# Two more key units of the first layer among the experts, and cross-attention weights forward in the ring

## The reference

```python
# first block, one layer
u = modulate(rmsnorm(h, g_norm1), sh1, sc1)
h = h + ga1 * hybrid_mixer(u, ...)               # convolution branch and gated linear attention
u2 = modulate(rmsnorm(h, g_norm2), sh2, sc2)
h = h + ga2 * hierarchical_moe(u2, ...)          # 32 experts: (silu(t @ w1) * (t @ w3)) @ w2, two a row
x = modulate(rmsnorm(h, g_final), shf, scf)
# second block, for each of its two layers l
x = x + 0.5 * swiglu_ffn(rms_norm(x, ffn1_norm_g[l]), ...)
proj = rms_norm(x, mix_norm_g[l]) @ w_mix_in[l]  # rwkv7_time_mix and moba_attention on its columns
x = x + concatenate([y_rwkv, y_moba]) @ w_mix_out[l]
# memory_cross_attention; mem_n = rms_norm(mem, mem_norm_g[l]), mem is an input of 256 rows
q = rms_norm(x, xattn_norm_g[l]) @ w_q[l]
k, v = jnp.split(mem_n @ w_kv[l], 2, axis=-1)    # 4 heads of 256
x = x + (softmax(q @ k.T / 16) @ v) @ w_o[l]
x = x + 0.5 * swiglu_ffn(rms_norm(x, ffn2_norm_g[l]), ...)
```

## Time and profile before

| | us |
|---|---|
| median of 3 runs | 2267.16 (2261.84 to 2268.1) |
| the profiled execution | 2264.74 |
| its span in the trace | 2262.9 |
| TensorE busy (PE) | 2182.5, 96% of the span |
| TensorE weight load (PEld) | 1481.2, 65% |
| VectorE (DVE) | 1240.8, 55% |
| ScalarE (ACT) | 424.7, 19% |
| GpSimd (POOL) | 47.5, 2% |

### The profile page before, as it was taken

How to read it: one execution, slowest core, us unless ns; L and a number is a source line. 1 busy time by engine, 2 the same in 40 slices (tenths; PEclk the granted TensorE clock), 3 DMA queues, 4 the chain that set the end, 5 groups by cost and what they waited for, 6 DMA issues and landing times.

```text
span 2262.9 us, 29955 instructions
## 1 busy us (share of the span) xinstructions
PE 2182.5 (96%) x12564; PEld 1481.2 (65%) x12564; DVE 1240.8 (55%) x2258; ACT 424.7 (19%) x852; POOL 47.5 (2%) x79
## 2 busy tenths in 40 slices
PE   7999999999999889999999999999999999999998
PEld 5778853333333338857978768857884966687873
DVE  2798432100011146667576766676666867667675
ACT  1123321100000012101232321102210132322110
POOL 1000100000000000000000000000000000000000
PEclk9999999999999999999999999999999999999999
DMA  9656579999999985444341435436443441245441
GB/s 406 266 225 257 223 212 381 422 421 421 422 422 421 422 323 174 161 167 171 123 154 50 149 126 182 155 124 223 161 175 130 168 150 57 78 150 183 159 181 42
DMA packets 174716, 499.94 MB, mean 221 GB/s; under 512 B 7016, under 2 KB 99448, under 8 KB 144384
## 3 DMA queue, kind: packets, MB, share of 16 engines
q1 hardware_dynamic: 170416, 481.23, 56.4%
q0 software_dynamic: 4032, 16.43, 2.3%
q10 hardware_dynamic: 144, 0.52, 0.1%
HBM read 491.34 MB, written 6.82 MB: 220 GB/s over the span
## 4 chain that ended last, share of the span: by engine, by line
PE 84%; DMA 12%; DVE 2%; issue 1%; ACT 0%; SPq 0%; POOL 0%; DVEq 0%; POOLq 0%
PE bank L2487 23%; PE bank L2535 11%; DMA ring<-in_w 10%; PE bank L939 6%; PE bank L2600 6%; PE bank L1512 6%; PE bank L3030 2%; PE bank L1553 2%; PE bank L2848 2%; PE bank L3103 2%; PE bank L2705 2%; PE bank L1602 1%; PE bank L2711 1%; PE bank L929 1%; PE bank L1043 1%; PE bank L1074 1%
## 5 line engine op out<-in xcount | busy, mean ns | idle before, releaser
L2487 PE MATMUL bank<-Tw,Sx 128*128 128x256 f32 x1032 | 229.9, 379 | 0.0
L2487 PEld LDWEIGHTS bank<-Tw,Sx 128*128 128x128 f32 x1032 | 193.0, 190 | 24.6
L1969 DVE TENSOR_TENSOR sg<-sg,bank 128x512 f32<-128x512 f32 x16 | 11.0, 687 | 273.7 <-PE bank L1512 273.7
L2487 PE MATMUL bank<-ring,xT 128*128 128x256 f32 x688 | 155.5, 379 | 0.0
L2487 PEld LDWEIGHTS bank<-ring,xT 128*128 128x128 f32 x688 | 130.5, 190 | 18.0 <-issue 0.5
L939 PE MATMUL bank<-xT,ring 128*128 128x256 f32 x640 | 141.8, 380 | 0.0
L1512 PE MATMUL bank<-ring,xg 128*64 128x512 f32 x512 | 115.0, 595 | 23.7 <-DMA ring<-in_w 23.7
L939 PEld LDWEIGHTS bank<-xT,ring 128*128 128x128 f32 x640 | 120.7, 190 | 19.0 <-issue 3.3
L1512 PE MATMUL bank<-more,xg 128*64 128x512 f32 x512 | 115.1, 596 | 16.8 <-DMA more<-in_w 16.0
L1553 PE MATMUL bank<-ring,hTg 128*64 128x512 f32 x512 | 113.5, 595 | 0.0
L3527 DVE TENSOR_TENSOR whole<-bank,part 128x256 f32<-128x256 f32 (+1 forms) x133 | 57.4, 432 | 99.4 <-PE bank L2487 98.1
(11 more groups left out here) (640 smaller groups left out, 3679.2 us busy)
## 6 DMA issues: line engine op xcount, KB each, us to landing
ring<-in_w SPq DMA_DIRECT2D x128, 1024.0 KB, 23.6
ring<-in_ffn_w_in SPq DMA_DIRECT2D x88, 1024.0 KB, 7.7
ring<-in_first_pieces SPq DMA_DIRECT2D x33, 2048.0 KB, 12.8
more<-in_w SPq DMA_DIRECT2D x64, 1024.0 KB, 23.5
ring<-in_ffn_w_out SPq DMA_DIRECT2D x20, 2048.0 KB, 7.8
ring<-in_w_mix_in SPq DMA_DIRECT2D x12, 2048.0 KB, 7.8
ring<-in_xattn_w_kv SPq DMA_DIRECT2D x6, 2048.0 KB, 8.0
ring<-in_w_mix_out SPq DMA_DIRECT2D x4, 2048.0 KB, 15.9
```

The lines of the kernel that those rows point to most:

```text
L2487: last = nc.tensor.matmul(bank[BANK_OF[name]][:, 0:SEQ], lhs(k), rhs(k), start=(k == 0), stop=(k == 3))
```

## The change

Units 0 and 1 of layer 0 are made in loop steps 1 and 2 of the experts, and layer 1's four key units move from steps 2 to 5 to steps 3 to 6. `LEFT` becomes [2, 3, 6, 7] in layer 0 and stays [4, 5, 6, 7] in layer 1. The key and value pieces that are left take the first two of their four places in the ring (24 and 25) in both layers, each piece's columns taken from `LEFT`, and 26 and 27 are skipped. There is a DRAM buffer of keys and one of values for each layer, in place of one of values, one of keys and one of early keys; the early units go to the layer's buffer, and the layer's own store writes only the columns that it made. Both buffers of a layer are read as before.

```diff
-EARLY = ((1, 0, 2), (1, 1, 3), (1, 2, 4), (1, 3, 5))
+EARLY = ((0, 0, 1), (0, 1, 2), (1, 0, 3), (1, 1, 4), (1, 2, 5), (1, 3, 6))
...
-        k_dram = nc.dram_tensor("cross_keys", (P, KD * SEQ), F32)
-        k_early = nc.dram_tensor("early_keys", (P, KD * SEQ), F32)
-        v_dram = nc.dram_tensor("cross_values", (P, NT * D), F32)
-        v_rows = v_dram.ap().rearrange("p (t d) -> p t d", t=NT)
+        k_dram = [nc.dram_tensor(f"cross_keys{l}", (P, KD * SEQ), F32) for l in range(DEPTH_2)]
+        v_dram = [nc.dram_tensor(f"cross_values{l}", (P, NT * D), F32) for l in range(DEPTH_2)]
+        v_rows = [v_dram[l].ap().rearrange("p (t d) -> p t d", t=NT) for l in range(DEPTH_2)]
...
-                if l == 1:
-                    pool.dma_start(k_early.ap()[:, g * 512:(g + 1) * 512], flat(early_out)).then_inc(early_moved, 16)
+                if g < 4:
+                    pool.dma_start(k_dram[l].ap()[:, g * 512:(g + 1) * 512], flat(early_out)).then_inc(early_moved, 16)
...
         def skipped(l, j):
-            return (j in J_SKIPPED or (l, j) == (0, J_VALUES)
-                    or J_KV <= j < J_KV + 4 and not any(cross_left(l, g) for g in (2 * (j - J_KV), 2 * (j - J_KV) + 1)))
+            return j in J_SKIPPED or J_KV + len(LEFT[l]) // 2 <= j < J_KV + 4
...
-                    sp.wait_ge(kv_psum, kv_done(l, 2 * (j - J_KV) + 1))
+                    sp.wait_ge(kv_psum, kv_done(l, LEFT[l][2 * (j - J_KV) + 1]))
...
-                mid += [(a["xattn_w_kv_2"], 512 * n, 512) for n in range(4)]
+                mid += [(a["xattn_w_kv_2"], 512 * (LEFT[l][2 * n] // 2 if 2 * n < len(LEFT[l]) else 0), 512)
+                        for n in range(4)]
...
-                if KEYS_LEFT[l]:
-                    pool.wait_ge(kv_act, kv_done(l, 3))
+                keys, values = LEFT[l][:KEYS_LEFT[l]], LEFT[l][KEYS_LEFT[l]:]
+                if keys:
+                    pool.wait_ge(kv_act, kv_done(l, keys[-1]))
                     pool.sem_inc(pool_passed, 1)
-                    pool.dma_start(k_dram.ap(), flat(k_out[:, :, :])).then_inc(k_stored, 16)
+                    pool.dma_start(k_dram[l].ap()[:, keys[0] * 512:(keys[-1] + 1) * 512],
+                                   flat(k_out[:, 2 * keys[0]:2 * keys[-1] + 2, :])).then_inc(k_stored, 16)
...
-                pool.dma_start(flat(kx[:, :, :]), (k_dram if KEYS_LEFT[l] else k_early).ap()).then_inc(kv_loaded, 16)
-                pool.dma_start(flat(vx[:, :, :]), v_dram.ap()).then_inc(kv_loaded, 16)
+                pool.dma_start(flat(kx[:, :, :]), k_dram[l].ap()).then_inc(kv_loaded, 16)
+                pool.dma_start(flat(vx[:, :, :]), v_dram[l].ap()).then_inc(kv_loaded, 16)
...
-                s = wait_piece2(pe, J_KV + g // 2, l)
+                s = wait_piece2(pe, J_KV + LEFT[l].index(g) // 2, l)
```

More of the change, by code:

```diff
@@ L157 @@
 EARLY_SEGMENTS = [_s for _s in _full if _s[0] < _s[1]]
-EARLY_COLUMNS = [(_l, _g * 256 if _g < 4 else D + 512 + (_g % 2) * 256) for _l, _g, _ in EARLY]
+EARLY_COLUMNS = [(_l, _g * 256 if _g < 4 else D + (_g // 2 - 2) * 512 + (_g % 2) * 256) for _l, _g, _ in EARLY]
 EARLY_LAYERS = list(dict.fromkeys(_l for _l, _, _ in EARLY))
@@ L824, in pool1 @@
             pool.wait_ge(kv_act, 2)
-            pool.dma_start(v_rows[:, :, 0:512], v_out[:, :, 0:512]).then_inc(v_stored, 16)
+            pool.dma_start(v_rows[0][:, :, 0:512], v_out[:, :, 0:512]).then_inc(v_stored, 16)
             pool.wait_ge(bd_stored, 16)
@@ L829, in pool1 @@
                 pool.wait_ge(early_act, u + 2 + EARLY_LAYERS.index(l))
-                if l == 1:
-                    pool.dma_start(k_early.ap()[:, g * 512:(g + 1) * 512], flat(early_out)).then_inc(early_moved, 16)
-                else:
-                    c = 512 + (g % 2) * 256
-                    pool.dma_start(v_rows[:, :, c:c + 256], early_out).then_inc(early_moved, 16)
+                if g < 4:
+                    pool.dma_start(k_dram[l].ap()[:, g * 512:(g + 1) * 512], flat(early_out)).then_inc(early_moved, 16)
+                else:
+                    c = (g // 2 - 2) * 512 + (g % 2) * 256
+                    pool.dma_start(v_rows[l][:, :, c:c + 256], early_out).then_inc(early_moved, 16)
         def tensor1(pe):
@@ L2042, in build @@
         J_SKIPPED = (51,)
-        J_VALUES = J_KV + 2
         assert PER_LAYER % SLOTS == 0 and J_MIX == FB + N_DOWN
@@ L2054, in build @@
         KEYS_LEFT = [sum(g < 4 for g in t) for t in LEFT]
-        assert all(n in (0, 4) for n in KEYS_LEFT)
+        assert all(t[0::2] == [g - 1 for g in t[1::2]] for t in LEFT)
         def keys_stored(l):
@@ L2410, in pool2 @@
                 norm_rstd(pool, l * 4 + 5)
-                if KEYS_LEFT[l]:
-                    pool.wait_ge(kv_act, kv_done(l, 3))
+                keys, values = LEFT[l][:KEYS_LEFT[l]], LEFT[l][KEYS_LEFT[l]:]
+                if keys:
+                    pool.wait_ge(kv_act, kv_done(l, keys[-1]))
                     pool.sem_inc(pool_passed, 1)
-                    pool.dma_start(k_dram.ap(), flat(k_out[:, :, :])).then_inc(k_stored, 16)
-                if len(LEFT[l]) > KEYS_LEFT[l]:
-                    pool.wait_ge(kv_act, kv_done(l, 7))
+                    pool.dma_start(k_dram[l].ap()[:, keys[0] * 512:(keys[-1] + 1) * 512],
+                                   flat(k_out[:, 2 * keys[0]:2 * keys[-1] + 2, :])).then_inc(k_stored, 16)
+                if values:
+                    pool.wait_ge(kv_act, kv_done(l, values[-1]))
                     pool.sem_inc(pool_passed, 1)
-                    columns = slice(512 if l == 0 else 0, D)
-                    pool.dma_start(v_rows[:, :, columns], v_out[:, :, columns]).then_inc(v_stored, 16)
+                    columns = slice((values[0] // 2 - 2) * 512, (values[-1] // 2 - 1) * 512)
+                    pool.dma_start(v_rows[l][:, :, columns], v_out[:, :, columns]).then_inc(v_stored, 16)
                 pool.wait_ge(k_stored, keys_stored(l))
```

## The result

The changed kernel takes 2270.37 us (median of 14 runs, 2267.72 to 2275.25), the kernel before 2266.62 us (14 runs, 2261.84 to 2269.9): ratio 1.0022, 95% interval 1.0014 to 1.0029. The forecast was 2260.0 with a range up to 2267. On a second chip, in experiment e5, the ratio was 1.0026 (1.0016 to 1.0036). So the change costs 4 to 6 us where 7 were to be gained.

A forecast was written before the change was run, and what follows sets the result against it. The DMA was taken to bound the expert stage (TensorE busy 96% overall). Terms 6.4 - 10.7 - 3.4 + 0.5 = -7.2 us took the profiled 2264.74 to 2257.5, median forecast 2260.0 us, range 2253.5 to 2267.

The forecast's parts named there:

- Term 1: Expert stage: two more early units cost only their DMA transfers, 3.2 us a unit, +6.4 us.
- rival B: Expert stage: the first new unit is not covered, 7.2 us in full instead of 3.2; total 2264 us, chance 0.16.
- Terms 2 and 3: Layer 0, line 2687 to line 2887: fewer units save 6.0 us up to line 2788, then 4.7; together -10.7 us.
- T: Start of the transposes at line 2687, the last work before a layer's first key and value unit.
- Term 4: Layer 1, line 2687 to line 2788: weights asked for earlier remove TensorE's wait and slow unit, -3.4 us.
- Term 5: Small products behind line 2887: output and query weights now transfer beside them, not waited for; instruction fetch costs +0.5 us.
- rival C: Small products from line 2887, both layers: moved weight transfers delay instruction fetches, up to 8.6 us; total 2268 us, chance 0.08.
- The prediction's own sign of error: Behind line 2887: the prediction is wrong if waits on "issue" grow past 2 us a layer.

The follow-up runs named there:

- e5: The changed kernel run again, unaltered, on a second chip, against the kernel before: 2271.21 us, ratio 1.0026.
- e7: The kernel before run again, unaltered, for a second profile: one run, 2264.01 us.
- e3: The kernel before with its second output piece held until the last key and value unit, no unit moved: 2274.32 us, ratio 1.0043 to the kernel before.
- e1: The changed kernel with the key and value weights in places 24 and 27 instead of 24 and 25: 2258.49 us, ratio 0.9972 to the kernel before.
- e2: The changed kernel with the queries' pieces asked for behind the inversions: 2264.97 us, ratio 0.9998 to the kernel before.
- e8: e1 run again on the second chip: 2260.1 us, ratio 0.9979 to the kernel before.

## Why the prediction was wrong

**Term 1, right.** +7.0 for +6.4 in this profile. From the down products of pair 3 (450.21) to those of pair 15 it is 373.70 us with five units: less 12 pairs of 29.83, 3.15 a unit, as forecast. The stretch with the first new unit grew by 4.0 us (99.66 from the stage's start to 450.21, against 95.65). The 7.17 us were not paid in full (rival B). The last down products did not stand at 819.8 since the stage began 3.5 us late.

**Terms 2 and 3, right.** The wait for the factors is 0.45 us (forecast 0.6), line 2788 comes at T + 27.7 (27.9), line 2887 at T + 53.5 (53.7): -10.8 for -10.7.

**Term 4, right in mechanism, its size in part by luck.** -3.5 for -3.4, no wait for the weights, full clock at 1850, and the two layers differ by 0.01 us. But the drop of the clock behind the wait, 1.8 us of it, was an accident of the one profile that the sum started from. In e7 and e3 it is absent behind waits of 2.48 and 2.39 us, and -1.7 is left.

**Term 5, wrong, and it decided the sign.** "What comes late next" found the transfers, their bytes and their time, and rightly that neither the store nor the weights would be waited for. Then it put +0.5 us on their running beside the small products. Measured: +5.35 and +5.4, so 10.7 us. That is rival C, named with its place, and given 0.08. The prediction's own sign of error, waits on issue past 2 us a layer, came with 4.5 and 6.1. The step that failed is how the cost was sized. The row against it, a wait of 0.19 us beside a 1 MB store, was a transfer that ends before the next block is due: all but one packet or two of it is through by 1906.0, and the block passes in the step from 1906.5. The upper bound, 1.44 us a fetch, was read from a row that shows no fetch. From 818 to 826 us no block passes on q8 in the kernel before, nor on either side of the same wait in the changed kernel (828.5 to 836), and the wait is 1.44 us in all ten profiles. What it is stays open. Measured, each late block cost 1.4 to 2.9 us: here the products use one up in under 4 us, and beside the weights the next comes 3 and then 2 us too late. And the clock, which dropped behind the longest waits, was in no term.

**Outside every term:** the dips in the first block, +3.5 us between the two profiled executions. The profile that the sum started from was one without them, 1.9 us below the median of 14 runs (2.4 below that of 3); so part of this is not in the difference of the medians.

With the terms as measured, 7.0 - 10.8 - 3.5 = -7.3 us for 1 to 4, and +10.7 for term 5 make +3.4, or +5.2 with the 1.7 us that term 4 is worth without the clock's accident; the medians say +3.8 on one chip and +6.0 on the other.

## What to carry to other kernels

When a change moves work away, read which transfers were released by it and where their issue goes now; then look at the instruction queue's packets in the stage that they land in. The stage of tiny products here, which takes a block of instructions every 3.5 to 4 us, had no slack for bulk transfers, even where nobody waited for their data. Issuing them earlier (e1) took the whole loss away, holding one of the two (e2) a part. A price for a fetch is to be taken only from a wait beside which a block passes, and a gain that has a clock drop in it only from more than one profile.

## What the hardware showed that was not expected

- A 16 KB block of TensorE's instructions, about 1 us long on its DMA engine with or without load, passed 3 us and then 5 us later than in e1 when two 2 MB transfers ran beside it (406 to 438 GB/s in the steps of the late blocks), and each late block cost TensorE 1.4 to 2.9 us.
- Behind the waits on issue of 2.67 us (layer 1 of the changed kernel) and 2.91 us (layer 0) TensorE ran at 1.2 GHz for some 3.5 us, and 60 of the small products took 2.89 us instead of 1.92. It isn't bound to follow: behind waits of 2.48 us (e7, 1849.76) and 2.39 us (e3) the clock stayed at 2.4 GHz.
- The clock fell to 1.2 GHz for some 3.5 us without any idle time of TensorE, in some executions and not in others, at 1.7 us a time. It came behind eight one-column products (line 875, 97.79 us) and eight of line 919, with TensorE busy throughout; e8 runs the same products in the same microseconds at full clock.
